# Four-layer sequence model on one core: where a relative bias is added, and where two attention maps are mixed

## The reference, cut to what matters

```python
q = rmsnorm(q, qn_g) * d ** -0.5 ; k = rmsnorm(k, kn_g)
sc = q @ k.T + rel_bias[h, clip(qpos - kpos, -256, 256) + 256]     # then the chunk mask
p = softmax(sc) ; o = p @ v
```

```python
o = softmax(q1 @ k1.T * s + causal) @ v - lam * (softmax(q2 @ k2.T * s + causal) @ v)
```

## Time and profile before

| | us |
|---|---|
| median of 3 runs (range) | 1983.82 (1981.48 to 1984.71) |
| the profiled execution, its own time | 1984.74 |
| its span in the trace | 1982.9 |
| PE busy | 1946.5 (98%) |
| DVE busy | 1165.8 (59%) |
| ACT busy | 1007.1 (51%) |
| POOL busy | 180.0 (9%) |
| mean granted clock of PE, 1.0 being 2.4 GHz | 0.991 |

### The profile page before, as it was taken

The page is one execution under the profiler, slowest core; times in us unless marked ns, Lnnn a source line. Parts: engine busy times, 40 slices in busy tenths (PEclk is TensorE's granted clock), DMA queues, the critical chain, the costliest instruction groups (busy, mean ns, idle before and its releaser), DMA issues.

```text
span 1982.9 us, 29116 instructions
## 1 busy us (share of the span) xinstructions
PE 1946.5 (98%) x12032; PEld 1750.4 (88%) x12032; DVE 1165.8 (59%) x1621; ACT 1007.1 (51%) x1543; POOL 180.0 (9%) x164
## 2 busy tenths in 40 slices
PE   8999999999999999989999999999999999999997
PEld 8988888888899989889899899888889989988886
DVE  5445554454556676778566556655556656654554
ACT  5345445654556545755553344456454344445643
POOL 0000010110003121301001001000000100100110
PEclk9999999999999999999999999999999999999999
DMA  7555555555554344444555654555555555455453
GB/s 265 170 191 170 170 191 176 159 166 180 187 163 139 128 139 139 148 129 157 183 180 191 194 171 146 167 183 165 175 186 183 178 191 168 152 191 170 164 198 128
DMA packets 172852, 338.52 MB, mean 171 GB/s; under 512 B 9536, under 2 KB 9920, under 8 KB 172592
## 3 DMA queue, kind: packets, MB, share of 16 engines
q1 hardware_dynamic: 171632, 332.89, 51.2%
q0 software_dynamic: 944, 3.61, 0.7%
q10 hardware_dynamic: 144, 0.16, 0.0%
HBM read 334.54 MB, written 2.10 MB: 170 GB/s over the span
## 4 chain that ended last, share of the span: by engine, by line
PE 94%; DVE 3%; ACT 1%; issue 1%; DMA 0%; SPq 0%; DVEq 0%; ACTq 0%
PE ACC L657 17%; PE ACC L655 17%; PE ACC L656 17%; PE ACC L662 11%; PE ACC L663 11%; PE ACC L664 11%; DVE WL L1266 1%; DVE S L1487 1%; PE PM L762 1%; PE PM L678 1%; PE PM L750 1%; PE PM L784 1%; PE PM L785 1%; PE PM L783 1%; ACT WH L958 1%
## 5 line engine op out<-in xcount | busy, mean ns | idle before, releaser
L1266 DVE TENSOR_TENSOR WL<-RAW,WH 128x1024 fp32r<-128x1024 f32 x624 | 788.5, 1277 | 630.2 <-ACT WH L958 628.6
L958 ACT ACTIVATE WH<-RAW 128x1024 fp32r<-128x1024 f32 x626 | 654.7, 1055 | 569.1 <-PE ACC L657 310.2
L662 PE MATMUL ACC<-XH,WH 128*128 128x256 f32 x1920 | 554.1, 289 | 4.6 <-DVE WL L1266 4.5
L663 PE MATMUL ACC<-XL,WH 128*128 128x256 f32 x1920 | 545.9, 284 | 0.0
L664 PE MATMUL ACC<-XH,WL 128*128 128x256 f32 x1920 | 545.6, 284 | 0.0
L655 PE MATMUL ACC<-WH,XH 128*128 128x512 f32 x1024 | 406.4, 397 | 0.0
L657 PE MATMUL ACC<-WH,XL 128*128 128x512 f32 x1024 | 399.0, 390 | 0.0
L656 PE MATMUL ACC<-WL,XH 128*128 128x512 f32 x1024 | 398.6, 389 | 0.0
L662 PEld LDWEIGHTS ACC<-XH,WH 128*128 128x128 f32 x1920 | 371.3, 193 | 7.0 <-DVE WL L1266 5.6
L663 PEld LDWEIGHTS ACC<-XL,WH 128*128 128x128 f32 x1920 | 371.2, 193 | 0.9
L664 PEld LDWEIGHTS ACC<-XH,WL 128*128 128x128 f32 x1920 | 371.0, 193 | 0.0
(11 more groups left out here) (327 smaller groups left out, 1704.9 us busy)
## 6 DMA issues: line engine op xcount, KB each, us to landing
RAW<-in_ev_w_in SPq DMA_DIRECT2D x71, 1024.0 KB, 4.9
RAW<-in_w_in_ab SPq DMA_DIRECT2D x64, 1024.0 KB, 5.5
RAW<-in_w_in_c SPq DMA_DIRECT2D x64, 1024.0 KB, 5.4
RAW<-in_od_w_in SPq DMA_DIRECT2D x48, 1024.0 KB, 5.1
RAW<-in_ev_w_out SPq DMA_DIRECT2D x16, 1024.0 KB, 4.9
RAW<-in_od_w_out SPq DMA_DIRECT2D x16, 1024.0 KB, 4.9
RAW<-in_w_out_ab SPq DMA_DIRECT2D x16, 1024.0 KB, 4.9
RAW<-in_w_out_c SPq DMA_DIRECT2D x16, 1024.0 KB, 4.9
```

Source lines behind the costliest of these rows:

```text
L662: e.matmul(o, wh, xh, start=f and g % 2 == 0, stop=False, skip_group_check=True)
L663: e.matmul(o, wh, xl, start=False, stop=False, skip_group_check=True)
L958: e.activation(hi, src, ACT.Copy).then_inc(s_hi)
L1266: e.tensor_tensor(lo, src, hi.bitcast(F32), ALU.subtract).then_inc(s_lo)
```

## The change

**Layer 0.** The bias comes from a table `bias` of 8 x 128 x 256 numbers, laid out by distance on the host. The matmuls with `flip` go, and the scores are two matmuls as in the other layers. DVE multiplies the scores by q's norm factor and adds the bias in one operation per row block, writing to SBUF; q is no longer scaled before. The bank is free after that operation and not after the exponentials. `flip` leaves the constants.

**Layer 2, the pairs.** The two maps of a pair are mixed before they are turned. `mix1`: DVE takes the reciprocals of both sums and multiplies the second by minus lam; ACT scales the first map by the first reciprocal, in place. `mix2`: DVE computes second map times factor plus first map. Then there is one `pT` and one `pv` for the pair, and ACT copies the result to Y and squares it. `pairs_plan` places these: with the even head's `scores` at slot s, the odd one's is at s+4, `mix1` at s+6, `mix2` at s+7, `pT` at s+8 and `pv` at s+12, the last two ahead of what else is there.

```diff
+        def pairs_plan(slot):
+            for a in range(8, 16):
+                put(slot + 4 * (a - 8), "scores", a, 1)
+            for i in range(4):
+                g = 4 + 9 + 2 * i
+                put(slot + 8 * i + 6, "mix1", i)
+                put(slot + 8 * i + 7, "mix2", i)
+                plan[slot + 8 * i + 8] = [("pT", g, 1)] + plan.get(slot + 8 * i + 8, [])
+                plan[slot + 8 * i + 12] = [("pv", g, 1)] + plan.get(slot + 8 * i + 12, [])
...
-            for i in range(4):
-                put(L(0, "ka", 1) + 3 + 3 * i, "scale_qk", i)
+            for i in range(2):
+                put(L(0, "ka", 1) + 3 + 3 * i, "scale_k", i)
...
-            heads_plan(first, L(layer, "v0", 1) + 2, 4)
+            if layer == 2:
+                pairs_plan(L(2, "v0", 1) + 2)
+            else:
+                heads_plan(first, L(layer, "v0", 1) + 2, 4)
...
# PE, scores
-                    for c, t, u in BLK:
-                        e.matmul(o[:, c:c + 128], qT[:, 128 * t:128 * t + 128], kT[:, 128 * u:128 * u + 128], start=True, stop=False)
-                        m = e.matmul(o[:, c:c + 128], bias[:, 128 * (t - u):128 * (t - u) + 128], con("flip"), start=False, stop=True)
-                    m.then_inc(s_sc)
...
+                o = bank(b)
+                e.matmul(o[:, 0:128], qT[:, 0:128], kT[:, 0:128], start=True, stop=True)
+                e.matmul(o[:, 128:384], qT[:, 128:256], kT, start=True, stop=True).then_inc(s_sc)
...
# PE, pT
+                    if is_diff(g - 4):
+                        e.wait_ge(*through(g - 4))
...
# ACT
+            def mix1(i, _):
+                p1, r1 = sc_slot(12 + 2 * i), cols(12 + 2 * i)[:, 2:4]
+                e.wait_ge(s_mix, 5 * i + 1)
+                e.activation(p1[:, 0:128], p1[:, 0:128], ACT.Copy, scale=r1[:, 0:1]).then_inc(s_mixA)
+                e.activation(p1[:, 128:384], p1[:, 128:384], ACT.Copy, scale=r1[:, 1:2]).then_inc(s_mixA)
...
# DVE, scores of layer 0
+                    e.scalar_tensor_tensor(sc[:, 0:128], PM[b][:, 0:128], ssA[0][:, 0, a:a + 1], bias[:, 128:256],
+                                           ALU.mult, ALU.add).then_inc(s_msk)
+                    e.scalar_tensor_tensor(sc[:, 128:384], PM[b][:, 128:384], ssA[0][:, 1, a:a + 1], bias,
+                                           ALU.mult, ALU.add).then_inc(s_msk)
...
# DVE
+            def mix1(i, _):
+                r1, r2 = cols(12 + 2 * i)[:, 2:4], cols(13 + 2 * i)[:, 2:4]
+                e.wait_ge(s_ex, 2 * (8 + 2 * i) + 4)
+                e.reciprocal(r1, r1).then_inc(s_mix)
+                e.reciprocal(r2, r2).then_inc(s_mix)
+                e.wait_ge(s_mix, 5 * i + 2)
+                e.tensor_scalar(r2, r2, lamc[:, 2:3], None, ALU.mult).then_inc(s_mix)
+
+            def mix2(i, _):
+                p1, p2, r2 = sc_slot(12 + 2 * i), sc_slot(13 + 2 * i), cols(13 + 2 * i)[:, 2:4]
+                e.wait_ge(s_mix, 5 * i + 3)
+                for t, c in enumerate((slice(0, 128), slice(128, 384))):
+                    e.wait_ge(s_mixA, 2 * i + 1 + t)
+                    e.scalar_tensor_tensor(p2[:, c], p2[:, c], r2[:, t:t + 1], p1[:, c], ALU.mult, ALU.add).then_inc(s_mix)
...
# POOL
-                e.dma_start(b, bass.AP(I["ev_rel_bias"].tensor, 513 * h + 129, [[1, 128], [1, 256]])).then_inc(s_bias[h % 2], 16)
+                e.dma_start(b, I["bias"][h]).then_inc(s_bias[h % 2], 16)
```

More of the change, by code:

```diff
@@ L335, in is_diff, with first_of_pair, masked @@
             return 8 <= a < 16
-        def by_vector(a):
-            return is_diff(a) and a % 2 == 1
-        HO = list(accumulate(0 if by_vector(a) else 2 for a in range(40)))
+        def first_of_pair(a):
+            return is_diff(a) and a % 2 == 0
+        HO = list(accumulate(0 if first_of_pair(a) else 2 for a in range(40)))
+        RC = list(accumulate(0 if is_diff(a) else 1 for a in range(40)))
+        TURN = list(accumulate(0 if g >= 4 and first_of_pair(g - 4) else 1 for g in range(44)))
+        def masked(a):
+            return 2 * a + 2 if a < 8 else a + 9
         plan = {}
@@ L522, in finished, with through @@
         def finished(a):
-            return (s_dif, 3 * ((a - 8) // 2) + 3) if by_vector(a) else (s_ho, HO[a])
+            return s_ho, HO[a]
+        def through(a):
+            return (s_mix, 5 * ((a - 8) // 2) + 5) if is_diff(a) else finished(a)
         def lc_at(half, level, u):
@@ L560, in program @@
         x_rows = I["x"].rearrange("(t p) c -> p t c", p=128)
[L561 removed]
+        n_id, n_cos, n_dil = COFF["ones"][0], COFF["cos"][0], COFF["dilated"][0]
         block = ctx.enter_context(nc.Block())
@@ L1073, in scores @@
                 sc, c = sc_slot(a + 4), cols(a + 4)
[L1074 to L1079, removed]
+                e.wait_ge(s_mx, 2 * a + 1)
+                e.activation(sc[:, 0:128], sc[:, 0:128], ACT.Exp, bias=c[:, 0:1], accum_out=c[:, 2:3]).then_inc(s_ex)
+                e.wait_ge(s_mx, 2 * a + 2)
+                e.activation(sc[:, 128:384], sc[:, 128:384], ACT.Exp, bias=c[:, 1:2], accum_out=c[:, 3:4]).then_inc(s_ex)
+            def mix1(i, _):
[3 more added lines that the diff above has]
+                e.activation(p1[:, 128:384], p1[:, 128:384], ACT.Copy, scale=r1[:, 1:2]).then_inc(s_mixA)
             def pv(g, b):
@@ L1085, in pv @@
                 layer, n, h = head_of(a)
-                if by_vector(a):
+                e.wait_ge(s_pv, TURN[g])
+                if is_diff(a):
+                    i = h // 2
                     for t in range(2):
[L1088 to L1093, removed]
+                        y = Y3[:, t, 1024 + 256 * i:1280 + 256 * i]
+                        e.activation(y, PM[b][:, 256 * t:256 * t + 256], ACT.Copy).then_inc(s_ho)
+                    for t in range(2):
+                        y = Y3[:, t, 1024 + 256 * i:1280 + 256 * i]
+                        e.wait_ge(s_ho, HO[a] - 1 + t)
+                        if i:
+                            e.wait_ge(s_dsq, 2 * i - 1 + t)
+                        e.activation(S6[:, 1024 + 256 * t:1280 + 256 * t], y, ACT.Square, accum_out=ss[:, t, i:i + 1]).then_inc(s_dsq)
                     return
[L1095 to L1098, removed]
+                at = (1024 if layer and n == 0 else 0) + 128 * h
+                e.wait_ge(s_rc, RC[a])
                 for t in range(2):
-                    e.activation(Y3[:, t, at:at + w], PM[b][:, w * t:w * t + w], ACT.Copy, scale=den[:, t:t + 1]).then_inc(s_ho)
+                    e.activation(Y3[:, t, at:at + 128], PM[b][:, 128 * t:128 * t + 128], ACT.Copy, scale=den[:, t:t + 1]).then_inc(s_ho)
             def ty(item, b):
@@ L1438, in pT @@
+            def mix2(i, _):
[4 more added lines that the diff above has]
+                    e.scalar_tensor_tensor(p2[:, c], p2[:, c], r2[:, t:t + 1], p1[:, c], ALU.mult, ALU.add).then_inc(s_mix)
             def pT(g, b):
-                if g >= 4:
+                if g >= 4 and not is_diff(g - 4):
@@ L1697, in vector @@
             steps = {"xt": xt, "rms_a": rms_a, "rms_b": rms_b, "gates1": gates1, "gates2": gates2, "decay_row": decay_row,
-                     "decay": decay, "mscores": mscores, "norm_qk": norm_qk, "scale_qk": scale_qk, "scores": scores, "pT": pT, "pv": pv,
+                     "decay": decay, "mscores": mscores, "norm_qk": norm_qk, "scale_k": scale_k, "scores": scores, "mix1": mix1,
+                     "mix2": mix2, "pT": pT, "pv": pv,
                      "finish": finish, "ty": ty, "conv": conv,
```

91 lines of the change are left out of this document (38 added, 53 removed).

## The result

The changed kernel takes 1987.09 us (median of 8 runs, 1986.0 to 1990.79); the kernel before took 1983.49 us on the same chips (8 runs, 1981.48 to 1984.71). The ratio is 1.0024, with a 95% interval of 1.0013 to 1.0035. So it is slower, by 2.6 to 6.9 us. 1988.6 us was predicted.

A forecast was written before the change was run, and what follows sets the result against it. PE, busy 98% of the span, was taken as the bound. -5.5 (layer 0) - 6.5 (pairs) + 10.8 (waits) + 6.0 (clock) = +4.8 us, giving 1988.6 us on the median's scale; own range 1985 to 1992, wider range 1981 to 1993.

The forecast's parts named there:

- layer 0 as a whole: Layer 0: PE's scores shorten by 0.69 us per head, times 8 heads, -5.5 us; everything else there 0.
- PE's work for the pairs: Layer 2's pairs: four turnings and four products with v go from PE, 4 x 1.63 = -6.5 us.
- four waits for the mixed map: Layer 2's pairs: PE stands still 2.7 us before each pair's turning, four times, +10.8 us; bounds 9.6 to 15.2.
- falls of the clock: PE's clock falls in three of the four gaps at the pairs, 2.0 us each, +6.0 us; bounds 0 to 10.8.
- PE as the bound: Both changed stretches: PE has no gap, so work removed from it, or a wait before it, counts fully as time.
- The wait: At each pair, a chain of 3.95 us follows DVE's evacuation, with 1.26 us left until PE asks for the map.
- The last pair: Fourth pair in layer 2: its gap a little longer than the others, since the blocks behind it have shorter slots.
- Rival 1: At the pairs, the waits come but the clock holds: -1.2 us, 1982.6 us, no change; chance 0.22.
- The range: The forecast's own range, whole kernel: 1985 to 1992 us, from waits of 9.6 to 11.5 and falls of 3 to 8.
- Rival 2: At the pairs, the mixed map is ready in time and the kernel is faster: -12.0 us, 1971.8 us; chance 0.12.
- Rival 3: At the pairs, POOL slows DVE in the chain: gaps of 3.8 us, falls in all four, 1995 us; chance 0.08.
- The sides taken at nothing: Layer 0's scalings, bias load and later exponentials (together -0.5 to +2 us), and the pairs' copies and squares: taken as 0.

The follow-up runs named there:

- e1: Kernel before with only the change of layer 0, the pairs as before; 1977.34 us, 0.9971 of the kernel before.
- e3: Changed kernel with mix1 one slot earlier (s+5) and mix2 at s+5.5, ahead of the rope block's evacuation; 1970.07 us, 0.9932 of the kernel before.
- e8: Changed kernel with two extra 256-column matmuls on PE ahead of the wait for the mixed map; 0.9993 of the kernel before.
- e5: Changed kernel with six extra 256-column matmuls on PE ahead of the wait for the mixed map; 1981.32 us, 0.9988 of the kernel before.
- e2: Kernel before with only the change of the pairs, layer 0 as before; 1.0055 of the kernel before, +10.9 us.
- e4: Changed kernel with the pair's turning (pT) one slot later on PE, mixing unmoved; 1970.88 us, 0.9931 of the kernel before.
- e6: Changed kernel with mix1 alone moved ahead of the evacuation (s+5.5), mix2 unmoved; 1977.52 us, 0.9965 of the kernel before.
- e7: Changed kernel with mix2 in mix1's slot, behind the evacuation but ahead of the next split; 1974.43 us, 0.9951 of the kernel before.
- e9: Changed kernel with one extra 256-column matmul on PE ahead of the wait for the mixed map; 1986.74 us, 1.0015 of the kernel before.

## Why the prediction was right, point by point

| step of the prediction | predicted, us | measured, us | by what |
|---|---|---|---|
| layer 0 as a whole | -5.5 | -5.5; -5.7 | its stretch in the traces; e1, 0.9971 |
| PE's work for the pairs | -6.5 | -6.5 | layer 2, e3 against before |
| four waits for the mixed map | +10.8 | +11.2, of which 10.4 idle | layer 2, e8 against e3; rows of the changed kernel |
| falls of the clock | +6.0 | +6.2; +7.1 | layer 2, changed kernel against e8; e5 by ratio |
| sum | +4.8 | +5.4 by these; +3.6 by medians, +4.8 by ratio | |

Stretches of the traces separate these terms, since each program has the same landmarks: DVE's first addition to X of each layer, here those of layers 1 and 2, before and after.

```profile
958.34 1.29 DVE L1298 TENSOR_TENSOR X<-ACC,X 128x512 f32<-128x512 f32 x2 [0.34 <-PE ACC L657]
1443.25 1.29 DVE L1298 TENSOR_TENSOR X<-ACC,X 128x512 f32<-128x512 f32 x2 [0.34 <-PE ACC L657]
...
953.56 0.69 DVE L1327 TENSOR_TENSOR X<-ACC,X 128x512 f32<-128x512 f32 x1 [0.34 <-PE ACC L682]
1449.38 1.29 DVE L1327 TENSOR_TENSOR X<-ACC,X 128x512 f32<-128x512 f32 x2 [0.34 <-PE ACC L682]
```

From landmark to landmark, in us, in the profiled execution of each kernel (layer 0 from the evacuation on DVE that starts at 279.77 us before):

| kernel | layer 0 | layer 1 | layer 2 | layer 3 |
|---|---|---|---|---|
| before | 216.65 | 461.92 | 484.91 | 479.88 |
| changed | 211.13 | 462.00 | 495.82 | 479.89 |
| e1 | 211.13 | 460.38 | 484.90 | 479.89 |
| e2 | 216.65 | 459.74 | 495.79 | 479.89 |
| e3 | 211.13 | 458.19 | 478.43 | 479.89 |
| e4 | 211.13 | 459.69 | 478.69 | 479.89 |
| e5 | 211.13 | 457.98 | 489.64 | 479.89 |
| e6 | 211.13 | 457.92 | 485.77 | 479.89 |
| e7 | 211.13 | 459.37 | 482.79 | 479.89 |
| e8 | 211.13 | 459.54 | 489.66 | 479.89 |
| e9 | 211.13 | 459.89 | 492.90 | 479.89 |

- **PE as the bound.** Right. The removed work counts in full: 5.52 us in layer 0 and 6.48 in layer 2 (e3). So does every gap: against e3, layer 2 is 4.4 us longer in e7 with 3.5 us of gaps, 7.3 in e6 with 6.5, 11.2 in e8. The whole times say the same less sharply, -9.7 us for e7, -6.9 for e6, -13.5 and -13.7 for e3 and e4, all 1.2 to 1.7 us below -12.0 plus their gaps.
- **What the whole times carry besides.** No edit touches layer 1, and yet it takes from 457.9 to 462.0 us, with the clock low for 17.1 us in e3, 27.3 in the kernel before and in the changed one, and 20.5 to 23.9 in the others. This can cover the 1.2 to 1.7 us, and it is why the sum of a few microseconds can't be read from whole times to better than one or two. With one profile of each kernel it stays open how far chance alone explains it.
- **The wait.** Right in its place, its cause and its size. The chain was put at 3.95 us behind the evacuation and took 1174.82 - 1170.87 = 3.95, each link within 0.1 us of its term (ACT's copies a little longer, its split a little shorter). The gap in brackets is 2.53 where 2.7 stood, because it counts from the end of the last matmul, and the prediction counted from where the next would have started. A product of 256 columns lasts 0.28 us and its successor starts 0.12 us after it, so counted by starts the wait is 0.16 us longer, 2.69 us.
- **The last pair.** The prediction's sum took all four alike, and its last part named the last one as a little longer: 2.81 us.
- **The clock.** The mechanism was right, the size by luck of two errors: four falls where three stood, and 1.5 to 1.7 us of loss each where I took 2.0. The low time was 3.4 us each where the rows of layer 1 had 6.8. Rival 1, the waits without falls, is out. The Trainium skill, page "TensorE: Matmul & The Clock Gate", section "HAM oscillation — how this bites in real kernels", warns only of longer idle gaps; the trace doesn't agree, since gaps of 2.53 us brought falls.
- **The range.** The forecast's own ends, waits of 9.6 to 11.5 and falls of 3 to 8, add up to 1984.4 and 1991.3 us, where 1985 to 1992 was written. Nothing hangs on it.
- **Rival 2**, the map in time, fell: it needed the split and ACT's copies away, as e3, e6 and e7 show by taking them away. **Rival 3**, POOL slowing DVE in the chain, did not come about in the changed kernel, since DVE was waiting for ACT while POOL added (its row of 1.10 us was off the chain); e6 and e7 show that it is there as soon as the order changes.
- **The sides taken at nothing** (scalings, bias load, later exponentials in layer 0, the squares of the pairs): nothing of them shows. e1 has no gap in layer 0.

The version to keep is e3 or e4; both beat the kernel before by 0.7% in whole time (in the edited layers 12.0 us for e3 and 11.7 for e4, 0.6%), and their whole times can't be told apart (intervals 0.9920 to 0.9945 and 0.9919 to 0.9944).

## What to carry to other kernels

Where one engine is busy without a gap, removed work counts in full, and so does every wait put ahead of it: before moving a step, look up in the other engines' queues what now stands ahead of each link of its chain, and add these from their rows; a large evacuation and a split between two links cost more here than all that the change removed from the pairs. If the sum is over the time left, ask one slot later or put the step ahead of the burst; both cost nothing here. A wait of 2.5 us on TensorE had a second price here, the fall of its clock, and one of 2.1 us had it sometimes; a few useless matmuls ahead of the wait avoided it where the wait itself stayed. And where an unedited layer varies by 4 us between profiled executions, compare the edited stretch between two landmarks of the traces and not only the whole time.

## What the hardware showed that I had not expected

- The clock's fall depends on more than the gap's length. In e8's profile gaps of 1.7 to 2.0 us brought none. In e9's, gaps of 2.10 us passed twice, and 2.09 and 2.39 didn't. Gaps of 2.53 and 2.8 us brought one in all eight cases, four in the changed kernel and four in e2. What else decides stays open.
- The low time behind one and the same gap is not fixed. It was 3.4 us each time at the pairs. Behind layer 1's gap of 4.33 us it was 6.8 us before, but in e5, behind 4.32 us, it was 0.90 + 1 + 1 + 0.52 = 3.4, from about 640.1:

```profile
640.00:641.00 1.00, 0.35 (x1) 0.55 0.60 229
...
643.00:644.00 1.00, 1.00 (x8) 0.74 0.00 0
```

- A DVE operation on two columns took 1.10 us in place of 0.23 beside a POOL addition, from 1171.17 to 1172.27. POOL's addition in the changed kernel:

```profile
1170.95 1.29 POOL L1806 TENSOR_TENSOR S<-S 128x512 f32<-128x512 f32 x1 [0.87 <-DVE S L1342]
```

It ends at 1172.24, and DVE's operation right behind it. The Trainium skill, page "SBUF — State Buffer", section "Who interferes with whom", says that VectorE and GpSimd share one pair of ports, and that where both need it the one that issues first holds it for its whole instruction while the other stands still. The trace agrees: 1172.24 and 1172.27. The two reciprocals beside the same addition took 0.17 and 0.15 us, as they did in e3 without one (0.16 and 0.15). In e6 the addition itself took 2.30 us in place of 1.29, beside a split that had started 0.05 us ahead of it.
